# Hybrid decoder step on one core: order of the opening (warm-up, sample and memory rows, turns)

## The chip, the cores and the metric

The kernel runs on 1 core of one Trainium2 chip. Its time is the device time of the execution in microseconds (us). Before the change it takes 1202.28 us, the median of 3 runs (1201.06 to 1202.86). The execution that was profiled took 1203.43 us, of which the profile's span covers 1201.6 us.

Names of the engines: PE is TensorE (PEld its weight loads), DVE is VectorE, ACT is ScalarE, POOL is GpSimd, SP is SyncE. SPq, ACTq and POOLq are their instruction streams where these issue DMAs.

## The reference

One layer of inference for 256 prompt rows with 16 memory ("meta") rows ahead of them, and for 8 sample rows of running sequences, all of 1024 columns in float32:

```
hp = concatenate([meta, x_prompt]);  hs = x_sample
u  = rmsnorm(h, norm_mix)
q, k, v, g, p, ga, gb = split(u @ w_in)            # w_in: 1024 x 5632
q, k = rotary(q), rotary(k) * dk ** -0.5
o, S_new = retention(q, k, v, S0)                  # 4 heads, chunks of 128
ya = (silu(g) * groupnorm(o)) @ w_ret_branch
yb = (pool_mix(p) @ pool_w * pool_scale) @ w_pool_branch
h  = h + (sigmoid(ga) * ya + sigmoid(gb) * yb) @ w_out
t  = rmsnorm(h, norm_ffn)
h  = h + sum over the top 4 of 32 experts of gate * ((up + 1) * glu(gate_part)) @ w_down
y  = rmsnorm(h, norm_final)
```

The outputs are the prompt's and the samples' rows, and the new retention and pooling states. The 32 experts hold 1024 x 2048 and 1024 x 1024 float32 weights each, about 400 MB, all of which are read.

## The kernel before, in words

All instructions are written out by hand, a block for each engine, with semaphores between the blocks; no scheduler moves anything. The order in which an engine's instructions stand in its block is the order in which it runs them.

The kernel has three stages. In the opening, three tiles of token rows are loaded into `tok`: `tok[:, 0]` and `tok[:, 1]` are the prompt's 2 x 128 rows, and `tok[0:24, 2]` the 8 sample and the 16 memory rows, the "few" rows (`few = NS + NM` is 24). TensorE turns them, 128 columns at a time, by a transpose against the identity `ident` (the first part of `consts`). ScalarE scales the turned prompt rows with `norm_mix` into `x_raw` (L1414, `raw_scaled`), VectorE does the same with the turned few rows (L1693, `few_scaled`). Beside that VectorE takes the row statistics of all three tiles (L1687, L1697) for the root mean squares, which are multiplied in later.

Then comes the mixer. Its projections and branches are 72 tiles of TensorE work (`for n in range(T_END)`), of 8 matmuls each (L1016), which take their weights from 4 units of SBUF that SP fills (L630; the first unit comes in two halves, L622 and L630). Tile n = 0 is the first with real work: its first matmul waits for `raw_scaled` (the first scaled prompt block), `few_scaled` and `part_in` (the first half of the first weights).

The last stage is the mixture of experts: 16 pairs of experts in a loop, whose weights stream through a ring of 9 slots in SBUF. SP issues the next load of a slot when TensorE has used what was in it (`used`, L670 before a load at L573, L576, L581).

What sets the order in the opening:
- SP issues the two prompt loads (L605), waits for `cleared` to reach 2, issues the sample and the memory rows (L607, L608), and then the weights (L622, L630).
- ScalarE issues the early constants with the identity (L1403) and four loads of small weights (L1405); then it runs a one-element Sqrt (L1409), ahead of which the activation table is loaded.
- GpSimd clears memory: `small`, `y_sums`, `tok[:, 2]` (1024 columns), `place`, `k_few` (128 columns), `q_only`. `cleared` counts the first and the third of them; `few_cleared` counts `k_few` first.
- TensorE waits for `few_cleared`, runs WARM = 6 matmuls on the cleared `k_few` whose result nobody reads (L938), waits for the identity, and then turns the prompt tile 0 (L945), `norm_mix` (L951), the prompt tile 1 (L945), and the few rows (L954).

Of the kernel before, what the change touches and what calls it, by code (L numbers as in the profile page):

```python
# [33 lines left out]
ALU = mybir.AluOpType  # L34
# [3 lines left out]
P = 128  # L38
D = 1024
KD = D // P  # L40
WARM = 6
NPR, NS, NM = 256, 8, 16
NT = NPR + NS
NA = NT + NM
# [219 lines left out]
def build(nc, ins, outs):  # L264
    x_prompt, x_sample, state_ret, state_pool, meta = (
        ins[n] for n in ("x_prompt", "x_sample", "state_ret", "state_pool", "meta_tokens"))
    y_prompt, y_sample, ret_prompt, pool_prompt, ret_sample, pool_sample = outs

    with ExitStack() as ctx:
# [21 lines left out]
        x_raw = ring[:, 0:KD * NA].rearrange("p (k t) -> p k t", k=KD)  # L291
# [45 lines left out]
        ident, ones = const("ident"), const("ones")  # L337
# [4 lines left out]
        norm_mix, gn_w, pool_scale, norm_ffn = (params[:, a:b] for a, b in ((0, 8), (8, 16), (16, 20), (20, 28)))  # L342
# [34 lines left out]
        tok = vk[:, 0:3 * D].rearrange("p (t d) -> p t d", t=3)  # L377
# [4 lines left out]
        v_few, k_few, k_meta = small_rows[:, 0:DV], small_rows[:, DV:DV + DK], small_rows[:, DV + DK:]  # L382
# [6 lines left out]
        rows = rs[:, 0:D]  # L389
# [54 lines left out]
        psum = ctx.enter_context(nc.psum_tensor("psum", [P, 8, 512], F32))  # L444
# [4 lines left out]
        def y_tok(t):  # L449
# [7 lines left out]
        x_in = [sem(f"x_in{t}") for t in range(3)]  # L457
        ident_in, consts_in, rows_in, hist_in, misc_in, final_in = (
            sem(n) for n in ("ident_in", "consts_in", "rows_in", "hist_in", "misc_in", "final_in"))
# [6 lines left out]
        cleared, sq_done, rms_done, rstd_ready, rstd_turned = (  # L466
            sem(n) for n in ("cleared", "sq_done", "rms_done", "rstd_ready", "rstd_turned"))
        params_turned, params_ready, x_turned, u_ready, kept = (
            sem(n) for n in ("params_turned", "params_ready", "x_turned", "u_ready", "kept"))
        norm_in, norm_turned, norm_ready, few_turned, raw_scaled, few_scaled, part_in = (  # L470
            sem(n) for n in ("norm_in", "norm_turned", "norm_ready", "few_turned", "raw_scaled", "few_scaled",
                             "part_in"))
        tile_done, act_took, dve_took = sem("tile_done"), sem("act_took"), sem("dve_took")
        aux_done, aux_took, roped = sem("aux_done"), sem("aux_took"), sem("roped")
        pooled_ready, k_meta_ready, few_cleared = (sem(n) for n in ("pooled_ready", "k_meta_ready", "few_cleared"))
# [122 lines left out]
        def _(sp):  # L598
# [4 lines left out]

            for t in range(2):
                sp.dma_start(tok[:, t, :], x_prompt[0, t * P:(t + 1) * P, :]).then_inc(x_in[t], 16)  # L605
            sp.wait_ge(cleared, 2)
            sp.dma_start(tok[0:NS, 2, :], x_sample.rearrange("b s d -> (b s) d")).then_inc(x_in[2], 16)  # L607
            sp.dma_start(tok[NS:NS + NM, 2, :], meta).then_inc(x_in[2], 16)  # L608

            def mix_chunk(i):  # L610
                kind, c = CHUNKS[i]
# [110 lines left out]
        @block.gpsimd  # L722
        def _(pool):
            step = Steps(pool, pool_step)
            nc.gpsimd.memset(small[:, 0:4], 1.0).then_inc(cleared, 1)
            nc.gpsimd.memset(y_sums, 0.0).then_inc(zeroed, 1)
            nc.gpsimd.memset(tok[:, 2, :], 0.0).then_inc(cleared, 1)
            nc.gpsimd.memset(place[:, :, :], FAR).then_inc(zeroed, 1)
            nc.gpsimd.memset(k_few[:, :], 0.0).then_inc(few_cleared, 1)
            nc.gpsimd.memset(q_only[:, :, :, :], 0.0).then_inc(few_cleared, 1)  # L730

            pool.wait_ge(wmix_in[0], 16)
# [44 lines left out]
            n = NM + NPR  # L777
# [43 lines left out]
        def _(pe):  # L821
# [119 lines left out]
            few = NS + NM  # L941
            for t in range(2):
                pe.wait_ge(x_in[t], 16)
                for k in range(KD):
                    last = pe.transpose(psum[:, 4 + k // 2, (2 * (k % 2) + t) * P:(2 * (k % 2) + t + 1) * P],  # L945
                                        tok[:, t, k * P:(k + 1) * P], ident)
                    if t == 1:
                        last.then_inc(x_turned, 1)
                if t == 0:
                    pe.wait_ge(norm_in, 16)  # L950
                    pe.transpose(psum[:, 2, 0:KD], rows[0:KD, 0:P], ident[0:KD, 0:KD]).then_inc(norm_turned, 1)  # L951
            pe.wait_ge(x_in[2], 32)
            for k in range(KD):
                last = pe.transpose(psum[:, 3, k * few:(k + 1) * few], tok[0:few, 2, k * P:(k + 1) * P],  # L954
                                    ident[0:few, 0:few])
            last.then_inc(few_turned, 1)

            def turn_roots():

# [9 lines left out]
            for n in range(T_END):  # L969
                if n >= 3:  # L970
                    wait_taken(pe, n - 3)
                o = psum[:, n % 3]
# [13 lines left out]
                elif n < T_YA:  # L986
                    d = n - T_YB
                    i, cols, x, width, nk = C_PB + d // 4, (d % 4) * P, pooled, NT, PG
                    w = unit(8 + i % MIX_SLOTS).rearrange("p (k n) -> p k n", k=PG)
                else:  # L990
                    d = n - (T_YA if n < T_OUT else T_OUT)
# [407 lines left out]
        def _(act_e):  # L1399
# [1 line left out]
            A = nc.scalar.activation  # L1401

            act_e.dma_start(consts[:, 0:EARLY], ins["consts"][:, 0:EARLY]).then_inc(ident_in, 16)  # L1403
            for o, name, n in ((0, "norm_mix", 8), (8, "ret_gn", 8), (16, "pool_scale", 4), (20, "norm_ffn", 8)):
                act_e.dma_start(rows[o:o + n, 0:P], ins[name].rearrange("l (a p) -> (l a) p", p=P)).then_inc(  # L1405
                    rows_in if o else norm_in, 16)

            act_e.wait_ge(cleared, 1)
            step(A(small[:, 1:2], small[:, 0:1], ACT.Sqrt))  # L1409

            act_e.wait_ge(norm_ready, 1)
# [182 lines left out]
        def _(dve):  # L1594
            V = nc.vector
# [88 lines left out]
            for t in range(2):  # L1684
# [3 lines left out]
                if t == 0:  # L1688
                    dve.wait_ge(norm_turned, 1)
                    V.tensor_copy(norm_mix, psum[:, 2, 0:KD]).then_inc(norm_ready, 1)  # L1690
            dve.wait_ge(norm_ready, 1)
            dve.wait_ge(few_turned, 1)
            V.tensor_tensor(x_raw[:, :, NPR:NA], psum[:, 3, 0:KD * few].rearrange("p (k c) -> p k c", k=KD),  # L1693
                            norm_mix.rearrange("p (k c) -> p k c", c=1).broadcast_to([P, KD, few]),
                            ALU.mult).then_inc(few_scaled, 1)
            for n in range(2):
                step(V.bn_stats(row_stats[:, 2, n], tok[:, 2, n * 512:(n + 1) * 512]))  # L1697
            step.wait()
# [370 lines left out]
```

## Time and profile before

| | |
|---|---|
| time, median of 3 runs | 1202.28 us (1201.06 to 1202.86) |
| time of the profiled execution | 1203.43 us |
| its span | 1201.6 us |
| PE busy | 1154.7 us, 96% |
| PE weight loads | 572.8 us, 48% |
| DVE, ACT, POOL busy | 307.2, 160.0, 62.8 us |
| chain that ended last | PE 68%, DMA 30%, SPq 1% |
| DMA over the span | 455.09 MB, mean 379 GB/s |

The busy times are shares of the whole span and say little of a stage of 9 us. For the opening the useful views are the chain of waits (what released what, up to the last instruction) and the timeline (each engine's instructions in order of time); for the rest, a table by stretches, which gives each engine's busy time, TensorE's granted clock (PEclk, 1.00 is full speed) and the share and rate of the DMA engines. In these views "idle 0.57 <-DMA ..." says that the engine had stood still for 0.57 us and what is taken to have released it.

### The profile page before, as it was taken

What the parts mean: (1) busy time and instruction counts of PE and PEld (TensorE: products, weight loads), DVE (VectorE), ACT (ScalarE), POOL (GpSimd) and SP (SyncE); (2) the same over time, 40 slices, a digit from 0 to 9 for tenths busy, and PEclk for the clock granted to TensorE, in tenths of its full rate; (3) what the DMA queues carried; (4) which work ended last, traced back from release to release, by engine and by line L of the source; (5) the groups of instructions that cost most, each with busy time, mean ns of one, the idle gap of its engine ahead of it and who ended that gap; (6) DMA issues with size and microseconds to landing.
All of it is one profiled execution on the core that took longest, in us unless ns stands there. A gap on an engine that the chain in (4) does not pass through costs nothing.

```text
span 1201.6 us, 13661 instructions
## 1 busy us (share of the span) xinstructions
PE 1154.7 (96%) x5403; PEld 572.8 (48%) x5403; DVE 307.2 (26%) x699; ACT 160.0 (13%) x314; POOL 62.8 (5%) x92
## 2 busy tenths in 40 slices
PE   8999999999999999999989998989999989999997
PEld 7888788886434334333434333434333434333332
DVE  4363511232122122221221221213121212121222
ACT  2122111002010111111110101010101100110112
POOL 3252600000000000000000000000000000000000
PEclk9999999999999999999999999999999999999999
DMA  9762788476999999999999999999999999999996
GB/s 321 231 228 90 261 327 319 142 315 264 424 418 427 424 434 428 425 434 425 425 434 426 431 428 434 421 435 426 436 425 433 421 433 429 433 428 429 428 419 241
DMA packets 63728, 455.09 MB, mean 379 GB/s; under 512 B 4321, under 2 KB 35501, under 8 KB 42688
## 3 DMA queue, kind: packets, MB, share of 16 engines
q1 hardware_dynamic: 59168, 439.60, 88.3%
q0 software_dynamic: 4176, 14.34, 3.5%
q8 instruction: 27, 0.44, 0.2%
q10 hardware_dynamic: 344, 0.61, 0.1%
q14 instruction: 13, 0.11, 0.0%
HBM read 448.65 MB, written 6.11 MB: 378 GB/s over the span
## 4 chain that ended last, share of the span: by engine, by line
PE 68%; DMA 30%; SPq 1%; issue 0%; ACT 0%; DVE 0%; DVEq 0%; ACTq 0%
PE psum L1087 24%; DMA ring<-in_w_down 21%; PE psum L1016 19%; PE psum L1098 10%; DMA ring<-in_w_gate_up 8%; PE psum L1174 5%; PE psum L1208 2%; PE psum L1154 1%; SPq L591 1%; PE psum L1164 1%; PE psum L1209 1%; PE psum L1183 1%; DMA ring<-in_x_prompt 0%; PE psum L897 0%; PE psum L1088 0%
## 5 line engine op out<-in xcount | busy, mean ns | idle before, releaser
L1087 PE MATMUL psum<-ring,x_T 128*64 128x512 f32 x1004 | 455.7, 600 | 9.6 <-DMA ring<-in_w_gate_up 8.8
L1088 PE MATMUL psum<-ring,x_T 128*64 128x512 f32 x994 | 450.6, 600 | 0.0
L1087 PEld LDWEIGHTS psum<-ring,x_T 128*64 128x64 f32 x1004 | 131.0, 137 | 275.1 <-issue 252.4
L1098 PE MATMUL psum<-ring,act_T 128*64 128x512 f32 x960 | 216.0, 602 | 25.1 <-DMA ring<-in_w_down 25.1
L1016 PE MATMUL psum<-ring 128*128 128x264 f32 (+1 forms) x768 | 181.7, 392 | 0.6 <-DMA ring<-in_w_in 0.6
L1016 PEld LDWEIGHTS psum<-ring 128*128 128x128 f32 x768 | 143.2, 190 | 30.2 <-ACT qk L1445 2.1
L1098 PEld LDWEIGHTS psum<-ring,act_T 128*64 128x64 f32 x960 | 70.2, 138 | 159.4 <-issue 139.6
L1088 PEld LDWEIGHTS psum<-ring,x_T 128*64 128x64 f32 x994 | 129.6, 137 | 0.0
L1906 DVE TENSOR_TENSOR h_raw<-psum,params 128x512 f32<-128x512 f32 x32 | 22.1, 691 | 295.0 <-PE psum L1154 295.0
L1923 DVE TENSOR_TENSOR z_T<-z_T,psum 128x264 f32<-128x264 f32 x112 | 43.0, 425 | 205.5 <-PE psum L1209 205.5
L1174 PE MATMUL psum<-normed,one_hot 128*128 128x512 f32 x168 | 74.4, 592 | 0.0
L1504 ACT ACTIVATE h_raw<-h_raw 128x512 f32<-128x512 f32 x32 | 20.2, 631 | 251.5 <-DVE h_raw L1909 251.5
L1487 ACT COPY h_raw<-psum 128x512 f32<-128x512 f32 x32 | 18.8, 586 | 224.5 <-PE psum L1088 224.5
L1174 PEld LDWEIGHTS psum<-normed,one_hot 128*128 128x128 f32 x168 | 30.9, 190 | 33.5 <-issue 33.5
L1154 PEld LDWEIGHTS psum<-consts,h_raw 128*128 128x128 f32 x256 | 33.6, 211 | 26.4 <-issue 26.0
L1918 DVE SCALAR_TENSOR_TENSOR act_T<-h_raw 128x512 f32<-128x512 f32 x30 | 20.8, 692 | 91.5 <-PE psum L1098 84.0
L1208 PEld LDWEIGHTS psum<-hot_T,out_hi 128*128 128x128 f32 x112 | 21.0, 187 | 45.4 <-issue 45.4
L1496 ACT COPY h_raw<-psum 128x512 f32<-128x512 f32 x28 | 16.4, 586 | 183.0 <-PE psum L1174 183.0
L1154 PE MATMUL psum<-consts,h_raw 128*128 128x128 f32 x256 | 40.1, 298 | 0.0
L1825 DVE TENSOR_TENSOR x_T<-psum,small 128x256 f32<-128x256 f32 x64 | 25.5, 420 | 52.8 <-PE psum L1164 27.3
L1208 PE MATMUL psum<-hot_T,out_hi 128*128 128x264 f32 x112 | 35.4, 336 | 0.0
L1209 PE MATMUL psum<-hot_T,out_lo 128*128 128x264 f32 x112 | 29.4, 283 | 0.0
(268 smaller groups left out, 751.3 us busy)
## 6 DMA issues: line engine op xcount, KB each, us to landing
ring<-in_w_gate_up SPq DMA_DIRECT2D x32, 4096.0 KB, 31.7
ring<-in_w_gate_up SPq DMA_DIRECT2D x59, 2048.0 KB, 29.8
ring<-in_w_down SPq DMA_DIRECT2D x56, 2048.0 KB, 33.3
ring<-in_w_in SPq DMA_DIRECT2D x21, 1024.0 KB, 6.6
ring<-in_w_down SPq DMA_DIRECT2D x12, 1024.0 KB, 26.8
spare<-in_w_gate_up SPq DMA_DIRECT2D x5, 1280.0 KB, 36.8
out<-ring POOLq DMA_DIRECT2D x9, 512.0 KB, 9.5
ring<-in_state_ret POOLq DMA_DIRECT2D x8, 512.0 KB, 7.2
```

The source lines that it names most:

```text
L1016: last = mm(o[:, 0:width], w[:, k, cols:cols + P], x[:, k, 0:width], start=k == 0, stop=k == nk - 1)
L1087: mm(psum[0:CAP, 2 * j + n], x, gate, start=first, stop=final)
L1088: last = mm(psum[CAP:P, 2 * j + n], x, up, start=first, stop=final)
L1098: last = mm(psum[j * CAP:(j + 1) * CAP, 4 + n], hidden[:, j, 4 * h + i], w, start=h == 0 and i == 0, stop=h == 1 and i == 3)
L1154: last = pe.transpose(psum[:, 6 + m // 4, (m % 4) * P:(m % 4 + 1) * P], h_raw[:, f0:f0 - m % 4 + 4 * P:4], ident)
L1174: last = mm(psum[:, bank + n], one_hot[:, t].rearrange("p j c -> p (j c)"), normed[:, t, n * 512:(n + 1) * 512], start=t == 0, stop=t == 2)
L1208: mm(o, out_hi[:, c], hot_T[:, :], start=True, stop=False)
L1209: mm(o, out_lo[:, c], hot_T[:, :], start=False, stop=True).then_inc(scattered, 1)
L1825: return V.tensor_tensor(x_T[:, k, j], psum[:, 4 + half].rearrange("p (k j c) -> p k j c", k=4, j=2)[:, :, j], ffn_pairs[:, k].rearrange(" ...
L1906: V.tensor_tensor(hg, turned[:, :, 0], bias(e, 0), ALU.add).then_inc(gate_biased, 1)
L1918: V.scalar_tensor_tensor(hidden[:, j], hu, 1.0, hs, ALU.add, ALU.mult).then_inc(act_ready, 1)
L1923: V.tensor_tensor(y_T[:, d], y_T[:, d], psum[:, 6 + d % 2, 0:NT], ALU.add).then_inc(y_added, 1)
```

## The change

- WARM goes from 6 to 10 matmuls, and GpSimd clears `k_few`, for which they wait, first of all instead of fifth. `tok[:, 2]` is cleared third as before, but behind `k_few` and `small` instead of `small` and `y_sums`.
- The sample and the memory rows are loaded from ScalarE's stream, behind the constants and `norm_mix`, instead of from SP's, ahead of the weights. ScalarE waits there for `cleared` to reach 2, and issues its three other small loads behind them.
- TensorE turns the few rows between the two prompt tiles instead of behind both, and VectorE scales them between the statistics of the two prompt tiles instead of behind both.

```diff
-WARM = 6
+WARM = 10
@@ SP
             for t in range(2):
                 sp.dma_start(tok[:, t, :], x_prompt[0, t * P:(t + 1) * P, :]).then_inc(x_in[t], 16)
-            sp.wait_ge(cleared, 2)
-            sp.dma_start(tok[0:NS, 2, :], x_sample.rearrange("b s d -> (b s) d")).then_inc(x_in[2], 16)
-            sp.dma_start(tok[NS:NS + NM, 2, :], meta).then_inc(x_in[2], 16)
@@ GpSimd
+            nc.gpsimd.memset(k_few[:, :], 0.0).then_inc(few_cleared, 1)
             nc.gpsimd.memset(small[:, 0:4], 1.0).then_inc(cleared, 1)
+            nc.gpsimd.memset(tok[:, 2, :], 0.0).then_inc(cleared, 1)
             nc.gpsimd.memset(y_sums, 0.0).then_inc(zeroed, 1)
-            nc.gpsimd.memset(tok[:, 2, :], 0.0).then_inc(cleared, 1)
             nc.gpsimd.memset(place[:, :, :], FAR).then_inc(zeroed, 1)
-            nc.gpsimd.memset(k_few[:, :], 0.0).then_inc(few_cleared, 1)
             nc.gpsimd.memset(q_only[:, :, :, :], 0.0).then_inc(few_cleared, 1)
@@ TensorE, in the loop over the two prompt tiles
                 if t == 0:
                     pe.wait_ge(norm_in, 16)
                     pe.transpose(psum[:, 2, 0:KD], rows[0:KD, 0:P], ident[0:KD, 0:KD]).then_inc(norm_turned, 1)
-            pe.wait_ge(x_in[2], 32)
-            for k in range(KD):
-                last = pe.transpose(psum[:, 3, k * few:(k + 1) * few], tok[0:few, 2, k * P:(k + 1) * P],
-                                    ident[0:few, 0:few])
-            last.then_inc(few_turned, 1)
+                    pe.wait_ge(x_in[2], 32)
+                    for k in range(KD):
+                        last = pe.transpose(psum[:, 3, k * few:(k + 1) * few], tok[0:few, 2, k * P:(k + 1) * P],
+                                            ident[0:few, 0:few])
+                    last.then_inc(few_turned, 1)
@@ ScalarE
-            for o, name, n in ((0, "norm_mix", 8), (8, "ret_gn", 8), (16, "pool_scale", 4), (20, "norm_ffn", 8)):
-                act_e.dma_start(rows[o:o + n, 0:P], ...).then_inc(rows_in if o else norm_in, 16)
-
-            act_e.wait_ge(cleared, 1)
+            act_e.dma_start(rows[0:8, 0:P], ins["norm_mix"]...).then_inc(norm_in, 16)
+            act_e.wait_ge(cleared, 2)
+            act_e.dma_start(tok[0:NS, 2, :], x_sample.rearrange("b s d -> (b s) d")).then_inc(x_in[2], 16)
+            act_e.dma_start(tok[NS:NS + NM, 2, :], meta).then_inc(x_in[2], 16)
+            for o, name, n in ((8, "ret_gn", 8), (16, "pool_scale", 4), (20, "norm_ffn", 8)):
+                act_e.dma_start(rows[o:o + n, 0:P], ...).then_inc(rows_in, 16)
             step(A(small[:, 1:2], small[:, 0:1], ACT.Sqrt))
@@ VectorE, in the loop over the two prompt tiles
                 if t == 0:
                     dve.wait_ge(norm_turned, 1)
                     V.tensor_copy(norm_mix, psum[:, 2, 0:KD]).then_inc(norm_ready, 1)
-            dve.wait_ge(norm_ready, 1)
-            dve.wait_ge(few_turned, 1)
-            V.tensor_tensor(x_raw[:, :, NPR:NA], ...).then_inc(few_scaled, 1)
+                    dve.wait_ge(norm_ready, 1)
+                    dve.wait_ge(few_turned, 1)
+                    V.tensor_tensor(x_raw[:, :, NPR:NA], ...).then_inc(few_scaled, 1)
```

On TensorE, at the program's start, the order before is this; the 128x24 matmuls are the turns of the few rows, the 128x280 ones are the first projections:

```order
1 L938 MATMUL psum<-ring 128x128 x6
2 L945 MATMUL psum<-consts,ring 128x128 x8
3 L951 MATMUL psum<-consts,ring 128x8
4 L945 MATMUL psum<-consts,ring 128x128 x8
5 L954 MATMUL psum<-consts,ring 128x24 x8
6 L1016 MATMUL psum<-ring 128x280 x16
```

And this is the order in the changed kernel, where each line number is 3 lower:

```order
1 L935 MATMUL psum<-ring 128x128 x10
2 L942 MATMUL psum<-consts,ring 128x128 x8
3 L948 MATMUL psum<-consts,ring 128x8
4 L951 MATMUL psum<-consts,ring 128x24 x8
5 L942 MATMUL psum<-consts,ring 128x128 x8
6 L1013 MATMUL psum<-ring 128x280 x16
```

The eight turns of the few rows have moved ahead of the second prompt tile, with their wait for the rows' landing, and four warm-up matmuls are new.

On ScalarE, at the program's start, the stream before is this:

```order
1 L1403 DMA consts<-in_consts 128x132
2 L1405 DMA ring<-in_norm_mix 8x128
3 L1405 DMA ring<-in_ret_gn 8x128
4 L1405 DMA ring<-in_pool_scale 4x128
5 L1405 DMA ring<-in_norm_ffn 8x128
6 L1409 ACT_TABLE_LOAD
7 L1409 ACTIVATE small<-small 128x1
8 L1414 ACTIVATE ring<-psum,params 128x256 x8
```

And this is the changed kernel's:

```order
1 L1400 DMA consts<-in_consts 128x132
2 L1401 DMA ring<-in_norm_mix 8x128
3 L1403 DMA ring<-in_x_sample 8x1024
4 L1404 DMA ring<-in_meta_tokens 16x1024
5 L1406 DMA ring<-in_ret_gn 8x128
6 L1406 DMA ring<-in_pool_scale 4x128
7 L1406 DMA ring<-in_norm_ffn 8x128
8 L1408 ACT_TABLE_LOAD
```

Two more DMAs are issued ahead of the table load, and both rows' loads stand behind the constants and `norm_mix`.

## Rows read from the trace of the kernel before

**Rows 1.** Chain of waits, 0 to 80 us: start us, us, what.

```profile
1.21 5.58 DMA ring<-in_x_prompt
...
6.84 1.09 PE psum L945 x8
7.93 0.60 PE psum L954 x8
...
9.10 7.79 PE psum L1016 x32
```

**Rows 2.** Timeline, 0 to 11 us: start us, us, engine, line, instruction, idle before.

```profile
0.75 0.10 POOL L725 MEMSET small<- 128x4 f32 x1 [0.29 <-POOLq L2061]
0.75 0.89 SPq L605 DMA_DIRECT2D ring<-in_x_prompt  x2
...
0.81 0.95 POOL L727 MEMSET ring<- 128x1024 f32 x1
...
1.79 0.34 SPq L607 DMA_DIRECT2D ring<-in_x_sample  x1
1.83 0.21 POOL L729 MEMSET ring<- 128x128 f32 x1
2.09 2.93 PE L938 MATMUL psum<-ring 128*128 128x128 f32 x12 [2.09 <-POOL ring L729]
...
2.18 0.33 SPq L608 DMA_DIRECT2D ring<-in_meta_tokens  x1
2.55 0.47 SPq L622 DMA_DIRECT2D ring<-in_w_in  x1
...
4.14 0.20 ACT L1409 ACTIVATE small<-small 128x1 f32<-128x1 f32 x1
4.97 1.29 DVE L1687 BATCH_NORM_STATS2 first_stats<-ring 128x6 f32<-128x512 f32 x2 [4.97 <-DMA ring<-in_x_prompt]
...
5.16 1.27 PE L945 MATMUL psum<-consts,ring 128*128 128x128 f32 x8
...
6.37 0.22 PE L951 MATMUL psum<-consts,ring 8*128 8x8 f32 x1
...
7.38 3.03 ACT L1414 ACTIVATE ring<-psum,params 128x256 f32<-128x256 f32 x8 [3.04 <-PE psum L945]
...
7.86 0.57 PEld L954 LDWEIGHTS psum<-consts,ring 24*128 24x128 f32 x8 [0.17 <-issue]
...
8.64 0.36 DVE L1693 TENSOR_TENSOR ring<-psum,params 128x192 f32<-128x192 f32 x1 [0.54 <-PE psum L954]
...
9.10 7.79 PE L1016 MATMUL psum<-ring 128*128 128x280 f32 x32 [0.57 <-DMA ring<-in_w_in]
```

**Rows 3.** The issue at L622 alone, and its time from issue to landing.

```profile
L622 SPq DMA_DIRECT2D ring<-in_w_in x1: 466/466/466, 2.5 to 2.5; - x1
DMA to landing us min/median/max: 6.0/6.0/6.0
```

**Rows 4.** DMA issues of 0 to 30 us: KB each, median us to landing.

```profile
consts<-in_consts ACTq DMA_DIRECT2D x1, 66.0 KB, 4.4
```

**Rows 5.** Warm-up and scaling alone: durations ns min/median/max, first and last start us.

```profile
L938 PE MATMUL psum<-ring x12: 421/421/582, 2.1 to 4.6; 128*128 128x128 f32 x12
L1414 ACT ACTIVATE ring<-psum,params x8: 468/488/516, 7.4 to 9.9; 128x256 f32<-128x256 f32 x8
```

**Rows 6.** By stretches: us, PE, PEld, DVE, ACT, POOL busy, PEclk, DMA share, GB/s.

```profile
5.50:6.50 1.00, 1.00 (x9) 0.83 (x7) 0.75 (x2) 0.00 (x0) 0.00 (x0) 1.00 1.03 237
6.50:9.00 2.50, 1.78 (x17) 1.42 (x16) 1.81 (x5) 1.62 (x5) 0.00 (x0) 1.00 1.08 343
260.00:280.00 20.00, 19.88 (x112) 16.31 (x110) 7.50 (x29) 4.05 (x6) 0.00 (x0) 0.91 0.65 263
285.00:290.00 5.00, 5.00 (x26) 1.60 (x24) 0.57 (x3) 0.00 (x0) 0.00 (x0) 1.00 0.32 82
300.00:1180.00 880.00, 845.41 (x3887) 330.36 (x3885) 201.48 (x437) 102.66 (x189) 0.00 (x0) 0.99 1.01 428
```

More of the change, by code:

```diff
@@ L1403, in _ @@
             act_e.dma_start(consts[:, 0:EARLY], ins["consts"][:, 0:EARLY]).then_inc(ident_in, 16)
-            for o, name, n in ((0, "norm_mix", 8), (8, "ret_gn", 8), (16, "pool_scale", 4), (20, "norm_ffn", 8)):
-                act_e.dma_start(rows[o:o + n, 0:P], ins[name].rearrange("l (a p) -> (l a) p", p=P)).then_inc(
-                    rows_in if o else norm_in, 16)
-            act_e.wait_ge(cleared, 1)
+            act_e.dma_start(rows[0:8, 0:P], ins["norm_mix"].rearrange("l (a p) -> (l a) p", p=P)).then_inc(norm_in, 16)
+            act_e.wait_ge(cleared, 2)
+            act_e.dma_start(tok[0:NS, 2, :], x_sample.rearrange("b s d -> (b s) d")).then_inc(x_in[2], 16)
+            act_e.dma_start(tok[NS:NS + NM, 2, :], meta).then_inc(x_in[2], 16)
+            for o, name, n in ((8, "ret_gn", 8), (16, "pool_scale", 4), (20, "norm_ffn", 8)):
+                act_e.dma_start(rows[o:o + n, 0:P], ins[name].rearrange("l (a p) -> (l a) p", p=P)).then_inc(rows_in, 16)
             step(A(small[:, 1:2], small[:, 0:1], ACT.Sqrt))
@@ L1690, in _ @@
                     V.tensor_copy(norm_mix, psum[:, 2, 0:KD]).then_inc(norm_ready, 1)
-            dve.wait_ge(norm_ready, 1)
-            dve.wait_ge(few_turned, 1)
-            V.tensor_tensor(x_raw[:, :, NPR:NA], psum[:, 3, 0:KD * few].rearrange("p (k c) -> p k c", k=KD),
-                            norm_mix.rearrange("p (k c) -> p k c", c=1).broadcast_to([P, KD, few]),
-                            ALU.mult).then_inc(few_scaled, 1)
+                    dve.wait_ge(norm_ready, 1)
+                    dve.wait_ge(few_turned, 1)
+                    V.tensor_tensor(x_raw[:, :, NPR:NA], psum[:, 3, 0:KD * few].rearrange("p (k c) -> p k c", k=KD),
+                                    norm_mix.rearrange("p (k c) -> p k c", c=1).broadcast_to([P, KD, few]),
+                                    ALU.mult).then_inc(few_scaled, 1)
             for n in range(2):
```

## The prediction

> **What bounds the kernel now.** I read the chain of waits first, then the timeline of the first 11 us, and then the table by stretches, because the change touches only the opening and the question is whether what happens there reaches the end.
>
> In the chain [rows 1] the reader sees that the opening hangs on the second prompt load: it lands at 6.79 us, TensorE turns tile 1 from 6.84 to 7.93 and the few rows to 8.53, stands still for 0.57 us and starts the projections at 9.10. From there TensorE works without a stop: the first two tiles of the projection take 7.79 us. What ended the 0.57 us has to be worked out. The view names the weights' DMA, but its landing was at 2.55 + 6.0 = 8.55 us [rows 2, 3], half a microsecond too early. VectorE's scaling of the few rows ran from 8.64 to 9.00 [rows 2], and TensorE started 0.10 us after it. ScalarE's first scaled block was done much sooner: it began at 7.38 and one takes 0.49 us, so 7.87 [rows 2, 5]. So three things had to be there, at 7.87, 8.55 and 9.00 us, and the few rows' scaling was the last.
>
> The rest of the program falls in two parts. The mixer up to about 280 us is TensorE's (19.88 us busy of 20 from 260 to 280), and from 285 to 290 the DMA engines are busy for only 0.32 of the time, because they wait for TensorE to free slots. From 300 to 1180 us the DMA share is 1.01 at 428 GB/s [rows 6]: the weights' stream is the limit. The stream's start, however, hangs on TensorE's progress through the mixer. So what the opening gains or loses moves the stream, and with it the end, by the same amount; I cost this passing-on at one for one.
>
> **The change part by part.**
>
> *SP's stream.* Two issues go, 0.34 and 0.33 us with their gaps. L622 was issued at 2.55 us, behind the row loads at 1.79 and 2.18, and the two prompt loads were issued from 0.75 to 1.64. So L622 moves to about 1.67, that is 0.88 us sooner [rows 2]. Does the landing move as much? At most: 8.55 - 0.88 = 7.67 us. At least hardly at all, since the transfers stand behind 1 MB of prompt rows of the same queue and the DMA engines are full (share 1.03 from 5.5 to 6.5). But the rate there is only 237 GB/s against 343 in the next stretch [rows 6], so something other than bytes holds the beginning of these transfers up. I take 0.3 us sooner, 8.25, nearer to no movement; the ends are 7.67 and 8.55.
>
> The Trainium skill, "DMA: Bandwidth & Descriptors", section "Issuing engines are not separate DMA queues", says that issuing from several engines saves only the issuing time, since all use the same 16 DMA engines. By that rule the gain is the issue time of SP alone and the bytes are not faster; by the trace the issue is worth 0.88 us at most, and whether it counts is open.
>
> *The rows on ScalarE's stream.* `tok[:, 2]` is cleared behind `k_few` (0.21 us) instead of behind `small` and `y_sums`; the clearing of 0.95 us began at 0.81 and begins now near 1.0, so it ends near 1.95 [rows 2]. The two loads are issued at 2.0 and 2.35 us, 0.2 us later than before, done near 2.7. They are no longer behind the prompt rows in SP's queue but behind the constants. When they land, no row of before shows. The nearest rows are the constants, 4.4 us from issue to landing on this queue [rows 4], and the weights, 6.0 us [rows 3]. Counted from 2.7 these give 7.1 and 8.7 us. The two loads are 24 rows of 4 KB, 96 KB in all, which could as well land in 4 us like the prompt tile 0 of 512 KB, which VectorE had at 4.97 us [rows 2]. I take 6.7, ends 6.2 and 8.7. Against the prompt they cost something: 96 KB at 343 GB/s [rows 6] are 0.28 us, which tile 1 can land later than 6.79, so 7.07.
>
> The Trainium skill, same page, section "Queues, rings and completion order", says each DMA engine goes round the queues that have work, packet by packet. By that rule the rows are not held up by the prompt's bytes ahead of them, and the prompt pays for it; the trace of before has no 4 KB rows on ScalarE's queue that would test it.
>
> The three small loads of ScalarE behind them slip by some 0.9 us, and so does the table load: the Sqrt ended at 4.34 and ends now near 5.3. ScalarE's next work was at 7.38 [rows 2], so 2 us of its idle time cover it. If that cover were gone the whole 0.9 would count.
>
> *The warm-up.* It waits for `k_few`, cleared now at 0.75 + 0.21 = 0.96 us instead of 2.04, and starts at 1.0 instead of 2.09. Each fp32 matmul is two passes in the trace; 12 passes started between 2.1 and 4.6 us [rows 5], 0.23 us apart. Twenty passes keep TensorE until 1.0 + 20 x 0.22 = 5.4 us, if they run at the pace of before. Tile 0 was begun at 5.16 [rows 2], so it starts about 0.25 us later. The passes took 421 ns each while the turns of the same shape came at a quicker pace, so the engine still ran at the lower of its two levels in the warm-up; longer work before tile 0 can bring the rise forward and give the 0.25 us back, but nothing here shows it.
>
> *The turns.* Before, tile 0 from 5.16, `norm_mix` at 6.37, then waiting until 6.79 for tile 1. Now tile 0 from 5.4, `norm_mix` at 6.6, the few rows at 6.85 if they have landed (0.57 us of weight loads), tile 1 from 7.4. Tile 1 was turned from 6.84 and ScalarE followed at 7.38, 0.54 us behind [rows 1, 2]. So ScalarE begins at 7.95 and its first block is there at 8.44 [rows 5]. VectorE has the turned few rows at 7.6 and is done at 8.0.
>
> *Sum.* The three conditions of the first projection become 8.44 (was 7.87), 8.25 (was 8.55) and 8.0 (was 9.00). The last is now ScalarE's first block, and TensorE starts at 8.5 instead of 9.10: 0.6 us sooner. The ends: 7.9 with all well (the clock rises early, the rows land at 6.2: 1.2 us sooner), and, with the rows landed at 8.7, 8.7 + 0.57 + 0.54 + 0.49 + 0.1 = 10.4, 1.3 us later. Nothing behind it turns late: ScalarE makes a block every 0.38 us (3.03 / 8), TensorE uses one in 0.49 (7.79 / 16) [rows 1, 2].
>
> In the profiled execution that is 1203.43 - 0.6 = 1202.8 us. The median of the runs shown lies 1.15 below that execution, so I forecast 1202.28 - 0.6, **1201.7 us**.
>
> **The rivals.**
>
> *Nothing moves.* The weights' first half is held by bytes and lands at 8.5 as before, and the rows come near 7.3. TensorE then starts between 8.7 and 9.1. For it: DMA share 1.03 and 1.08 in these stretches [rows 6]. Against it: the few rows' scaling at 9.00 was later than both other conditions and does go. Gain 0 to 0.4, time 1202.1.
>
> *The rows block tile 1.* TensorE runs in order, so the wait for the few rows now stands ahead of tile 1, of ScalarE's eight blocks and of VectorE's statistics. The path from their landing to the start is 0.57 + 0.54 + 0.49 + 0.1 = 1.7 us, so from a landing later than 9.10 - 1.7 = 7.4 us the change loses. At 8.7 us it loses 1.3, time 1203.6. If TensorE's clock falls in that longer pause, there is more: from 260 to 280 us the granted clock was 0.91 [rows 6], which is 0.09 x 20 = 1.8 us of full-speed work lost; 1.3 + 1.8 = 3.1, time 1205.4. For it: the constants needed 4.4 us on this very queue. Against it: prompt tile 1, issued at 1.21 and 5 times larger, was there in 5.6 us.
>
> *The clock is worth more than the order.* The profiled execution is only one. If in others TensorE is still at its lower level when the projections begin, a longer warm-up mends that. For it: the three runs lie 1.8 us apart, and the warm-up's passes did run at the lower level. Against it: the same spread can come from the 880 us of streaming, of which 0.2% is already as much. Gain 0.6 + up to 1.8, 1199.9 to 1201; with 1.2 it is 1200.5.
>
> **How the numbers follow.** Forecast (0.3 to 1.2 sooner) 0.60; nothing moves 0.16; rows block tile 1 0.13, of which 0.04 with the clock; clock worth more 0.11, of which 0.07 go past the bound. A difference under 0.2%, 2.4 us, can't be told from none. So faster 0.07, slower 0.04, the same 0.89. The range takes the forecast's ends (1201.1 and 1202.0), then the spread of the runs, 1.2 down and 0.6 up from their median, and half of the clock's 1.8 on either side: 1199.8 to 1203.4.
>
> **What would show it.** Right: the first L1016 matmul (L1013 there) starts between 8.2 and 8.8 us; the warm-up starts near 1.0 and ends near 5.5; SP's first weight issue at 1.7; the Sqrt ends before ScalarE's first block; VectorE's scaling of the few rows ends by 8.1, and the whole chain is shifted alike at 280 us. Wrong: TensorE idle between `norm_mix` and the few rows beyond 7.4 us; a start of the projections at 9.1 or later; a gap at the fifth matmul of the first tile, where the second half of the weights is asked for; a gain at 9 us that is gone at 300 us, which would break the one-for-one passing-on.

## The result, and the profile after

The changed kernel takes 1204.24 us, the median of 20 runs (1202.26 to 1205.99), against 1202.19 us (1201.06 to 1202.96, 20 runs) before. The ratio is 1.0016, 95% interval 1.001 to 1.0022: about 2 us slower. The forecast was 1201.7 with a range up to 1203.4, so it was wrong in its sign, and the time lies outside the range. A second measurement of the same kernel, told below, gave 1.0025 (1.0015 to 1.0034).

The chain of waits of the changed kernel, 0 to 20 us (start us, us, what), answers to [rows 1]:

```profile
1.91 0.28 ACTq L1403
2.19 0.03 issue
2.22 6.11 DMA ring<-in_meta_tokens
8.33 0.04 issue
8.38 0.79 PE psum L951 x8
9.17 1.90 PE psum L942 x8
11.06 8.16 PE psum L1013 x32
19.22 0.77 PE psum L960 x6
```

The opening no longer hangs on the second prompt tile but on the memory rows. Their DMA was issued at 2.22 us on ScalarE's queue and landed at 8.33, 6.11 us later. TensorE stood still for it, with tile 1 behind it in its stream. The projections start at 10.86 us in the timeline below instead of 9.10 (the chain counts them from 11.06, when tile 1 is through), and their first two tiles end at 19.22 instead of 16.89. That is 2.33 us later, more than the start by 0.57.

The timeline of the changed kernel shows the same on each engine, and answers to [rows 2]:

```profile
1.00 4.56 PE L935 MATMUL psum<-ring 128*128 128x128 f32 x20 [1.00 <-POOL ring L722]
...
1.68 0.43 SPq L619 DMA_DIRECT2D ring<-in_w_in  x1
...
5.39 1.04 PE L942 MATMUL psum<-consts,ring 128*128 128x128 f32 x8
...
6.36 0.22 PE L948 MATMUL psum<-consts,ring 8*128 8x8 f32 x1
...
8.37 0.67 PEld L951 LDWEIGHTS psum<-consts,ring 24*128 24x128 f32 x8 [1.88 <-DMA ring<-in_meta_tokens]
...
9.10 1.97 PE L942 MATMUL psum<-consts,ring 128*128 128x128 f32 x8
...
9.28 0.36 DVE L1692 TENSOR_TENSOR ring<-psum,params 128x192 f32<-128x192 f32 x1 [2.49 <-PE psum L951]
...
9.89 3.02 ACT L1413 ACTIVATE ring<-psum,params 128x256 f32<-128x256 f32 x8 [4.56 <-PE psum L942]
...
10.86 8.37 PE L1013 MATMUL psum<-ring 128*128 128x280 f32 x32
```

The reader sees the pause in front of L951, 1.88 us, and that tile 1 (at 9.10) now takes 1.97 us for the eight turns that took 1.09 before [rows 1]. Tile 0 had taken 1.04. The by-stretch table (us, PE, PEld, DVE, ACT, POOL busy, PEclk, DMA share, GB/s) says why; it answers to [rows 6]:

```profile
6.00:8.50 2.50, 0.71 (x7) 0.46 (x6) 0.35 (x2) 0.00 (x0) 0.00 (x0) 1.00 1.10 272
8.50:10.00 1.50, 1.50 (x12) 1.45 (x13) 0.72 (x2) 0.11 (x1) 0.00 (x0) 0.59 1.10 348
10.00:12.50 2.50, 2.50 (x10) 2.10 (x10) 2.43 (x8) 2.50 (x8) 1.26 (x2) 0.56 1.10 349
12.50:19.00 6.50, 6.50 (x29) 5.28 (x28) 3.00 (x8) 1.08 (x4) 0.00 (x0) 1.00 1.09 330
260.00:280.00 20.00, 20.00 (x125) 16.51 (x124) 7.00 (x27) 2.83 (x5) 0.00 (x0) 1.00 0.65 261
```

TensorE worked for 0.71 of the 2.5 us up to 8.50, and its granted clock was then 0.59 and 0.56 on average until 12.50: it had fallen to the lower of its two levels, 1.2 GHz instead of 2.4, for most of these 4 us, and was back at 1.00 behind them. Before, the column read 1.00 through the whole opening. It does so even during the warm-up, where TensorE was slow: these 20 passes took 4.56 us, 0.23 each, while the 8 unread passes of e9, told below, took 1.16 at 7 us, 0.15 each. So until the engine first runs at full pace, 1.00 in this column says nothing.

The weights' first half did not come sooner either: issued at 1.68 instead of 2.55 us, it took 7.1 us instead of 6.0 [rows 3], and landed at 8.8 instead of 8.55.

```profile
DMA to landing us min/median/max: 7.1/7.1/7.1
```

### The profile page after: what moved, and what is told of

The parts are those of the page before. It is cut to its first block, busy times and chain, and to the rows that moved or that the text cites. A ratio compares the mean times of both kernels' runs of the same rounds, so it can differ in the third digit from the quotient of the medians.

```text
span 1202.3 us, 13677 instructions
## 1 busy us (share of the span) xinstructions
PE 1155.6 (96%) x5411; PEld 575.4 (48%) x5411; DVE 307.3 (26%) x699; ACT 159.6 (13%) x314; POOL 62.6 (5%) x92
## 3 DMA queue, kind: packets, MB, share of 16 engines
HBM read 448.65 MB, written 6.11 MB: 378 GB/s over the span
## 4 chain that ended last, share of the span: by engine, by line
PE 67%; DMA 30%; SPq 1%; issue 0%; ACT 0%; DVE 0%; POOL 0%; ACTq 0%; DVEq 0%; POOLq 0%
PE psum L1084 23%; DMA ring<-in_w_down 22%; PE psum L1013 19%; PE psum L1095 11%; DMA ring<-in_w_gate_up 8%; PE psum L1171 5%; PE psum L1205 1%; PE psum L1151 1%; PE psum L1161 1%; SPq L591 1%; PE psum L1206 1%; PE psum L1180 1%; DMA ring<-in_meta_tokens 1%; PE psum L894 0%; PE psum L1085 0%
```

## The experiments

Eleven experiments ran, one of them the changed kernel again. A useful mark in each profile is the start of the 10.88 us stretch of three projection tiles near the mixer's end, since TensorE does not stop between the opening and there; it stood at 258.32 us before and at 260.67 in the changed kernel.

```profile
258.32 10.88 PE psum L1016 x48
```

```profile
260.67 10.88 PE psum L1013 x48
```

So 2.35 us separate the two, the 2.33 of the opening within rounding. The table holds what the profile of each kernel shows, and beside it the ratio of the times, whose interval is some 1 us either way. A mark is sharp, but it is that of one execution: the changed kernel was profiled twice, and its two marks differ by 0.65 us. So marks of a few tenths, taken from one profile each, show which way a change points and no more. The starts are those of the timelines.

| kernel | memory rows landed | projections start | mark against before | ratio (95%) |
|---|---|---|---|---|
| before | by 7.86 | 9.10 | 0 | 1 |
| changed | 8.33 | 10.86 | +2.35 | 1.0016 (1.0010 to 1.0022) |
| e8, changed again | 8.59 | 10.39 | +3.00 | 1.0025 (1.0015 to 1.0034) |
| e1, warm-up alone | by 8.20 | 9.45 | +0.36 | 1.0001 (0.9988 to 1.0013) |
| e2, rows on SP | 7.0 | 8.79 | -0.30 | 1.0003 (0.9993 to 1.0012) |
| e3, turned last | 8.5 | 9.82 | +2.42 | 1.0007 (0.9998 to 1.0016) |
| e4, 5 fillers | 8.4 | 10.21 | +1.12 | 1.0013 (1.0004 to 1.0022) |
| e9, 4 fillers | 8.39 | 10.19 | +1.10 | 1.0016 (1.0007 to 1.0025) |
| e4b, 7 fillers | before 9.12 | 10.88 | +1.79 | 1.0017 (1.0008 to 1.0026) |
| e5, rows on GpSimd | 8.89 | 10.84 | +2.98 | 1.0019 (1.0011 to 1.0028) |
| e6, constants on SP | 7.5 | 9.39 | +0.33 | 1.0003 (0.9994 to 1.0011) |
| e7, turned in tile 1 | by 7.48 | 8.79 | -0.37 | 0.9994 (0.9985 to 1.0003) |
| e10, the same, 8 warm-ups | 7.08 | 8.44 | -0.64 | 0.9995 (0.9986 to 1.0004) |

**e1, the warm-up alone.** The kernel before, with

```diff
-WARM = 6
+WARM = 10
+            nc.gpsimd.memset(k_few[:, :], 0.0).then_inc(few_cleared, 1)
             nc.gpsimd.memset(small[:, 0:4], 1.0).then_inc(cleared, 1)
-            nc.gpsimd.memset(k_few[:, :], 0.0).then_inc(few_cleared, 1)
```

> The kernel before with the warm-up's part of the change alone (k_few cleared first, ten matmuls). My theory, that the loss comes from the few rows landing late ahead of tile 1 and from the clock that falls in that pause: projections start at 9.1 us as before, granted clock 1.00 from 6 to 19 us, time within 0.4 us of before. Rival, the longer warm-up itself is the loss (it delays tile 0 or makes the granted clock fall later on): start later than 9.5 us or a clock under 1.00 before 19 us, and 1 to 2 us slower.

The ratio was 1.0001 (0.9988 to 1.0013). In its timeline:

```profile
1.00 4.64 PE L938 MATMUL psum<-ring 128*128 128x128 f32 x20 [1.00 <-POOL ring L725]
...
5.43 1.66 PE L945 MATMUL psum<-consts,ring 128*128 128x128 f32 x8
...
7.17 1.09 PE L945 MATMUL psum<-consts,ring 128*128 128x128 f32 x8
...
9.45 7.79 PE L1016 MATMUL psum<-ring 128*128 128x280 f32 x32 [0.57 <-issue]
```

Ten warm-ups keep TensorE until 5.43, tile 0 starts 0.27 us late and was still slow in this execution (1.66 us), so that tile 1 was begun at 7.17 instead of 6.84 and the start slipped by 0.35. The warm-up alone brought nothing and cost little: with a mark at +0.36 it is not the loss of 2.35. From 8.5 to 19 us the clock was 1.00. The start at 9.45 is later than my 9.1, and just short of the rival's 9.5.

**e2, the rows back on SP's queue.** The changed kernel, with

```diff
+            sp.wait_ge(cleared, 2)
+            sp.dma_start(tok[0:NS, 2, :], x_sample...).then_inc(x_in[2], 16)
+            sp.dma_start(tok[NS:NS + NM, 2, :], meta).then_inc(x_in[2], 16)
@@ ScalarE
-            act_e.wait_ge(cleared, 2)
-            act_e.dma_start(tok[0:NS, 2, :], x_sample...).then_inc(x_in[2], 16)
-            act_e.dma_start(tok[NS:NS + NM, 2, :], meta).then_inc(x_in[2], 16)
+            act_e.wait_ge(cleared, 1)
```

> The changed kernel with the sample and memory rows' two loads put back into SP's stream, behind the prompt and ahead of the weights; warm-up and the turn between the two tiles stay. Theory (ScalarE's queue makes the rows late): they land near 7.3 us, TensorE idles at most 0.7 us, projections start at 8.9 to 9.1, clock 1.00, time 0 to 0.3 us under before. Rival (turning the few rows between the tiles costs by itself, whoever loads them): rows at 8 us or later, start after 10 us, 1.5 to 2 us slower than before.

Ratio 1.0003 (0.9993 to 1.0012), and in the timeline:

```profile
2.28 0.33 SPq L608 DMA_DIRECT2D ring<-in_meta_tokens  x1
...
5.06 1.09 PE L945 MATMUL psum<-consts,ring 128*128 128x128 f32 x8
...
7.03 0.57 PEld L954 LDWEIGHTS psum<-consts,ring 24*128 24x128 f32 x8 [0.81 <-DMA ring<-in_meta_tokens]
...
8.79 7.79 PE L1016 MATMUL psum<-ring 128*128 128x280 f32 x32
```

Issued at about the same time as in the changed kernel, but behind the prompt on SP's queue, the rows were there at 7.0 instead of 8.33 us. All came a little sooner than expected (7.3 us, start 8.9 to 9.1), and the turn between the tiles gives 0.3 us. This takes the loss away by undoing one part, so the moved loads are its cause. That part holds two things: the rows leave ScalarE's queue, and they are issued ahead of the weights again (SP issues the first weights at 2.65 us instead of 1.68). No run separates them; a kernel with the rows on ScalarE's queue and the weights held back behind them would, and was not run.

**e3, the few rows turned last again.** The changed kernel with TensorE's turn and VectorE's scaling of the few rows put back behind both prompt tiles:

```diff
-                    pe.wait_ge(x_in[2], 32)      (in the loop, behind norm_mix)
+            pe.wait_ge(x_in[2], 32)              (behind the loop, with its eight turns; the same on VectorE)
```

> The changed kernel with the few rows turned and scaled behind both prompt tiles, as before; their loads stay on ScalarE's queue. Theory: rows land at 8.3 us, tile 1 is turned from 6.9 to 8.0 meanwhile, the few rows to 9.0, scaled at 9.6, start at 9.7 with the clock at 1.00; 0.6 us slower than before. Rival (the place of the turn doesn't matter, the late rows cost the same wherever they are waited for): start at 10.5 or later, 2 us slower.

Ratio 1.0007 (0.9998 to 1.0016), near the 0.6 us expected; the start at 9.82 is near the 9.7 expected. But the clock was not at 1.00 in the profiled execution, which was the slowest of the kernel's eleven runs (1205.38 us, median 1203.03):

```profile
6.11 1.09 PE L942 MATMUL psum<-consts,ring 128*128 128x128 f32 x8
...
8.58 0.57 PEld L951 LDWEIGHTS psum<-consts,ring 24*128 24x128 f32 x8 [1.62 <-DMA ring<-in_meta_tokens]
...
9.82 9.47 PE L1013 MATMUL psum<-ring 128*128 128x280 f32 x32 [0.57 <-issue]
```

The first two projection tiles took 9.47 us instead of 7.79: 1.7 us for one fall of the clock behind a pause of 1.6 us. This execution was 2.35 us over the kernel's median, and it also had the other fall, of 1.50 us, told in the last section. So at least one of the two was missing in most of its runs, and which one is not known; the forecast of 1.00 for the opening missed in the one execution that was seen. By the way tile 1 was turned at 6.11, 0.7 us sooner than before. Whether the prompt lands sooner because the few rows are gone from its queue was not tried; with them on it, e10 began tile 1 at 6.51.

**e4, e9 and e4b, TensorE kept at work in the pause.** The changed kernel, with unread matmuls ahead of the wait:

```diff
+                    for _ in range(5):
+                        mm(psum[:, 7, 0:P], k_few, k_few, start=True, stop=True)
                     pe.wait_ge(x_in[2], 32)
```

In e4 they write over a part of the turned prompt tile 0 in PSUM, so that its computation differs in those columns; e9 (four) and e4b (seven) write to bank 1 and leave all as it is.

> The changed kernel with five more unread 128x128 matmuls between the turn of norm_mix and the wait for the few rows, so that TensorE works through the pause. Theory, that about half of the loss is the clock: rows at 8.3 us as before it, granted clock 1.00 from 8.5 to 12.5 us, projections start at 10.1 to 10.4 and their first two tiles take 7.8 us; 1.1 us slower than before, 0.9 faster than the changed kernel. Rival (the wait alone is the loss): the clock may be up, but the time is the changed kernel's within 0.3 us.

> The changed kernel with seven unread 128x128 matmuls in the pause ahead of the few rows (into a PSUM bank that holds nothing yet). Measured so far: with a filler the projections start at 10.21 us and run at full clock, the first two tiles done at 18.0 us, against 19.2 in the changed kernel and 16.9 before. Theory (the opening passes on one for one): 1.1 us slower than before, 0.9 to 1.2 faster than the changed kernel's 2.05. Rival (the time lost is not the opening's): 2 us slower although the opening is 1.2 us shorter.

> The changed kernel with four unread matmuls in the pause, short enough to end before the rows land. Theory (of the 2 us about one is the clock): projections start at 10.0 to 10.3 us at full clock, first two tiles done at 18.0, 1.0 to 1.3 us slower than before, 0.8 to 1.2 faster than the changed kernel beside it. Rival (the clock costs nothing in the whole time): the same time as the changed kernel within 0.3 us.

In e9's timeline:

```profile
6.98 1.16 PE L950 MATMUL psum<-ring 128*128 128x128 f32 x8
...
8.43 0.57 PEld L953 LDWEIGHTS psum<-consts,ring 24*128 24x128 f32 x8 [0.49 <-DMA ring<-in_meta_tokens]
...
9.04 1.09 PE L942 MATMUL psum<-consts,ring 128*128 128x128 f32 x8
...
10.19 7.79 PE L1015 MATMUL psum<-ring 128*128 128x280 f32 x32
```

The rows came as late as ever, but the clock was 1.00 in all four stretches from 6 to 19 us, tile 1 took 1.09 and the projections 7.79. The mark stood at +1.10 and in e4 at +1.12, against +2.35 and +3.00 without fillers. So of the changed kernel's delay at the mark 1.1 us is the wait. The rest is 1.25 us in its first profile and 1.90 in its second (e8), where 0.20 us are the rows' later landing; that leaves 1.2 to 1.7 us for the clock.

In the times this gain does not show. e9's ratio 1.0016 lies below the 1.0025 of the changed kernel measured beside it (medians 1204.24 and 1205.04, the intervals overlap), but it equals the 1.0016 of that kernel's first 20 runs. The traces say where the gain can go: all three kernels with fillers had the other fall of the clock, behind the mark (last section), and neither profile of the changed kernel had it. SP's first load for the experts behind it was issued at 288.50 us in the changed kernel's first profile, and here at

```profile
288.76 3.76 SPq L576 DMA_DIRECT2D ring<-in_w_gate_up  x2
```

The 1.25 us won at the mark were gone 29 us later. So the rival of e4's forecast, that the clock may be up and the time the same, is not ruled out, and the 0.8 to 1.2 us expected of e9 were not shown.

e4b missed: its seven fillers began at 7.36, since the warm-up and tile 0 had been slow in that execution, and held TensorE until 9.12, beyond the rows' landing; the mark +1.79 fits the ratio 1.0017. It does not test what I sent it for.

**e5, the rows on GpSimd's queue.**

```diff
             nc.gpsimd.memset(tok[:, 2, :], 0.0).then_inc(cleared, 1)
+            pool.wait_ge(cleared, 2)
+            pool.dma_start(tok[0:NS, 2, :], x_sample...).then_inc(x_in[2], 16)
+            pool.dma_start(tok[NS:NS + NM, 2, :], meta).then_inc(x_in[2], 16)
```

> The changed kernel with the few rows' two loads issued by GpSimd right behind its own clearing. Theory, that the rows are late because they stand behind the constants and norm_mix on ScalarE's queue: on another queue they land by 7.0 us and the projections start by 9.0; time within 0.5 us of before. Rival, that any second queue is starved beside the prompt and the weights: landing at 8 us or later, start after 10 us, 1 to 2 us slower.

The rival's numbers held: landing at 8.89 us, start at 10.84. The chain:

```profile
2.82 6.07 DMA ring<-in_meta_tokens
```

Only the sample rows stood ahead of the memory rows on that queue, and they still took 6.07 us, against 6.11 on ScalarE's and 4.7 (2.28 to 7.0) on SP's. Projections from 10.84 in 9.01 us, with the clock at 0.51 from 10 to 12.5 us, ratio 1.0019. Two things keep it from being a clean test of "any second queue": the profile lists this queue as another kind (software_dynamic, the other two are hardware_dynamic), and SP's weights were still issued ahead of the rows, at 1.68 us.

**e6, the constants off ScalarE's queue.**

```diff
                 sp.dma_start(tok[:, t, :], x_prompt...).then_inc(x_in[t], 16)
+                if t == 0:
+                    sp.dma_start(consts[:, 0:EARLY], ins["consts"][:, 0:EARLY]).then_inc(ident_in, 16)
@@ ScalarE
-            act_e.dma_start(consts[:, 0:EARLY], ins["consts"][:, 0:EARLY]).then_inc(ident_in, 16)
```

> The changed kernel with the early constants issued by SP between the two prompt tiles; ScalarE's queue then holds norm_mix, the few rows and the three small loads. Theory (backlog of the constants' 128 small rows on ScalarE's queue): rows land by 6.5 us, identity by 5.5, start at 8.5 to 9.0 us, 0.3 us faster than before. Rival (a queue beside SP's gets its transfers late whatever stands ahead of them): rows land at 8 us or later, 1 to 2 us slower.

```profile
2.14 0.43 SPq L621 DMA_DIRECT2D ring<-in_w_in  x1
...
2.23 0.34 ACTq L1405 DMA_DIRECT2D ring<-in_meta_tokens  x1
...
7.59 0.57 PEld L953 LDWEIGHTS psum<-consts,ring 24*128 24x128 f32 x8 [0.56 <-DMA ring<-in_meta_tokens]
...
9.39 7.81 PE L1015 MATMUL psum<-ring 128*128 128x280 f32 x32
```

Between the two: the rows landed near 7.5 us, 5.3 after the issue. That is 0.8 us sooner than in the changed kernel, of which not all need be the constants: SP issued the weights 0.46 us later here (2.14 against 1.68). And ScalarE's queue still takes 0.6 us longer than SP's. Here the weights, landed at 2.14 + 7.20 = 9.34 us, set the start. The packets by queue tell where the time went. In the changed kernel ScalarE's queue (q10) moved nothing from 4.6 to 5.5 us, while SP's (q1) moved 0.34 MB, and the 0.10 MB of the rows, issued by 2.6 us, ran from 5.5 to 7.5. In e6, with no constants ahead, q10 had moved 0.07 MB of them by 5.5. So the rows' first bytes start late behind the constants, and their last ones are slow beside the weights in both. Why a queue beside SP's takes longer is left open. In the profiles of before, of the changed kernel and of e1, e2 and e3 the DMA engines are full between 6 and 7 us (shares 1.02 to 1.14) at only 252 to 264 GB/s, when the weights' small pieces begin; whether that is the reason was not tried.

**e7 and e10, the rows turned inside tile 1.** From the kernel before (rows on SP's queue), with e1's warm-up; the few rows are turned behind tile 1's first two turns, and VectorE scales them between tile 1's two statistics. e10 is the same with WARM = 8.

```diff
                     if t == 1:
                         last.then_inc(x_turned, 1)
+                    if t == 1 and k == 1:
+                        pe.wait_ge(x_in[2], 32)
+                        for j in range(KD): (the turns of the few rows)
+                        last.then_inc(few_turned, 1)
```

> The kernel before (rows on SP's queue) with the longer warm-up, and the few rows turned behind the first two turns of tile 1, whose scaling ScalarE starts at once. Theory: rows there by 7.1 us, tile 1's first two turns from 6.9, few rows turned by 7.9, start at 8.6 to 8.8, which the weights' landing (8.3 to 8.6) bounds; 0.3 to 0.5 us faster than before, not to be told from none. Rival (the start is bound by the weights' landing near 8.6 or the bytes): start between 8.9 and 9.4 as in the kernel before.

> The version with the few rows on SP's queue turned inside tile 1 (the one with ten warm-up matmuls started the projections at 8.79 us), now with eight. Theory, that ten overrun the identity's landing and push tile 1 from 6.8 to 7.1: tile 0 starts at 5.1, the projections at 8.5 to 8.7, 0.4 to 0.6 us faster than before. Rival, that eight end too early for the clock: granted clock under 1.00 between 6 and 13 us and a time 0 to 1 us over before.

e10's timeline:

```profile
4.90 1.52 PE L945 MATMUL psum<-consts,ring 128*128 128x128 f32 x8
...
6.51 0.44 PE L945 MATMUL psum<-consts,ring 128*128 128x128 f32 x2
...
7.12 0.57 PEld L952 LDWEIGHTS psum<-consts,ring 24*128 24x128 f32 x8 [0.41 <-DMA ring<-in_meta_tokens]
...
8.44 7.80 PE L1017 MATMUL psum<-ring 128*128 128x280 f32 x32
```

ScalarE's first two blocks go ahead and the few rows' wait hides behind them. The start moves to 8.79 and 8.44 us (expected 8.6 to 8.8, and 8.5 to 8.7), the mark to -0.37 and -0.64 us, both near what was expected. The ratios, 0.9994 and 0.9995, point the same way with 1 inside their intervals. By the mark it is the better kernel, in one profile each and by no more than two profiles of one kernel can differ (0.65 us); by the times it is not to be told from before.

**e8, the changed kernel again.**

> The changed kernel itself once more, for a second profile and beside e9 on one chip. Theory, that the late rows and the fall of the clock in the pause both recur: rows land at 8.2 to 8.4 us, granted clock under 1.00 somewhere between 8 and 13 us, the projections' first two tiles done at 18.8 to 19.3 us, 2 us slower than before. Rival, that the fall in the first profile was a chance of that execution: clock 1.00 to 19 us, first two tiles done at 17.9 to 18.2, time 1 to 1.3 us over before in most runs.

```profile
8.63 0.57 PEld L951 LDWEIGHTS psum<-consts,ring 24*128 24x128 f32 x8 [1.22 <-DMA ring<-in_meta_tokens]
...
9.24 1.09 PE L942 MATMUL psum<-consts,ring 128*128 128x128 f32 x8
...
10.39 9.47 PE L1013 MATMUL psum<-ring 128*128 128x280 f32 x32
```

The rows were late again (2.22 + 6.37 = 8.59 us) and the clock fell again, this time later: tile 1 took its full-speed 1.09 us and the projections 9.47. The mark was +3.00, the ratio 1.0025. The landing (expected by 8.4) and the end of the two tiles (19.86, expected by 19.3) were later than I had said. The rival is gone: the fall came in both profiles of this kernel, and its place moved. It begins between 8.5 and 9 us in the first and between 10.5 and 11 here, when TensorE had been at work again for about 2 us.

## Why the prediction was wrong

The chain was read rightly: before, the few rows' scaling, done at 9.00, was the last condition. In e1 it was done at 9.35 and the projections started at 9.45, again 0.10 us behind. That the opening's loss reaches the end one for one fits as far as the times can tell: in the changed kernel the mark has moved by 2.35 us and the time by 2.05 (20 runs), and in e8 by 3.00 and about 3.0. Between mark and end the clock's other fall can come in between (e9).

The step that failed is "The rows on ScalarE's stream". It put their landing at 6.7 us, with ends 6.2 and 8.7; it was 8.33 and 8.59, near the far end. The issue was costed well (2.22 us, against 2.35). What failed is the time from issue to landing. The 6.7 is 4.0 us behind the end of the issue at 2.7, or 4.35 behind its start: the figure of prompt tile 0 and of the constants (4.4 us), which were issued first, when the DMA engines had nothing else. It measured 6.11 from the start of the issue. The nearest row was the weights' 6.0 us [rows 3], issued at nearly the same time as the rows; with it the sum gives 2.35 + 6.0 = 8.35 and the slower outcome. I had the row and used it only for the far end. That the two figures agree so well is in part luck, since the weights themselves then took 7.1 us.

"The rows block tile 1" was the rival that came true, with a chance of 0.13, of which 0.04 with the clock. Its working holds: from landing to start 1.7 us, so 8.33 + 1.7 = 10.0, and e9 started at 10.19 with the rows at 8.39, which is 1.8. Its clock term, 1.8 us, was 1.2 to 1.7. The wait (1.1 us) and the clock add up to what the mark moved. The chance looks too small, above all for the clock, since a pause of nearly 2 us directly ahead of the work was plain once the landing was set late. The range did not hold this rival either: it ended at 1203.4, below the 1203.6 and 1205.4 that the rival gave, so 0.13 of the chances lay outside it. Its ends were also added up wrongly: from the terms named they are 1201.1 - 1.2 - 0.9 = 1199.0 and 1202.0 + 0.6 + 0.9 = 1203.5, not 1199.8 and 1203.4. The measured time lies outside either.

"SP's stream": I took the weights 0.3 us sooner between ends 7.67 and 8.55. They landed at 8.8, outside both. The issue came 0.87 us sooner and the transfer took 1.1 us longer. The rule of the Trainium skill, "DMA: Bandwidth & Descriptors", section "Issuing engines are not separate DMA queues", that issuing from several engines saves only the sequencer's time, agrees with the trace as far as it goes: the bytes came no sooner. Here even the 0.87 us of issuing that were saved were worth nothing at the landing. The prediction also drew on the Trainium skill, "DMA: Bandwidth & Descriptors", section "Queues, rings and completion order", by which each DMA engine takes the queues in turn, packet by packet. What I concluded from it, that the rows would not be held up off SP's queue, is not borne out as a gain: there they came 1.3 us later (e2 against the changed kernel).

"The warm-up" was sized rightly (start 1.00, tile 0 from 5.39, expected 5.4), and e1 shows it as a loss of 0.35 us in the opening, not as a gain, in one execution in which tile 0 was also slow (1.66 us). "The turns" were right too: with the rows there in time (7.0 us, e2) the order gives 0.3 us, where the sum had 0.6. The rival "the clock is worth more" found no support: before, in e1 and in e2 the clock was at its full level when the projections began.

## What to carry to other kernels

A small load that is moved to another queue and awaited earlier is not priced by its bytes: take the issue-to-landing time of what is issued beside it under the same load (here 6.0 us, against 6.11 measured), not of what was issued first (4.4). A wait moved ahead on an in-order engine should stand behind work that other engines are already waiting for (e7, e10), and a pause that it may open on TensorE is to be priced with the clock's fall, which at the mark cost as much as the pause itself. For changes under 0.2% a mark in the profile behind the changed part tells more than the times, but it wants more than one profile of each kernel (0.65 us between two here) and a second mark further on, since a gain at the first can be gone at the second (e9).

## What was not expected of the hardware

TensorE's clock also fell once between the mixer and the experts, in 6 of the 13 profiles, and no pause stood before it. In the profile of before TensorE was busy without a stop from 19 us on; from 271.6 to 274.3 it ran four groups of six matmuls of only 32 or 1 columns, then 24 turns (L1039), and the clock fell at about 275. In the profile before, the granted clock from 260 to 280 us was 0.91 [rows 6], in the changed kernel's 1.00. From the mark to SP's next load, which waits for TensorE's first expert work, it was 287.65 - 258.32 = 29.33 us before and 288.50 - 260.67 = 27.83 after:

```profile
287.65 3.76 SPq L576 DMA_DIRECT2D ring<-in_w_gate_up  x2
```

```profile
288.50 3.76 SPq L576 DMA_DIRECT2D ring<-in_w_gate_up  x2
```

The 1.50 us are that fall's price. The same step is 29.33 or 29.34 us in all six profiles with the fall (before, e2, e3, e4, e4b and e9) and 27.83 or 27.84 in all seven without it. What decides whether it comes is open. It came behind openings at full clock and behind one with a fall (e3), but in all three kernels with fillers and in neither profile of the changed one.

It explains why the two profiled executions lie only 0.84 us apart (1203.43 and 1204.27) though their openings differ by 2.33 us: 2.33 - 1.50 = 0.83. That the figures meet so closely is luck. From the load at 287.65 and 288.50 to the end it was 915.8 us in both, but over the thirteen profiled executions it was 914.3 to 916.8, so the experts' stream adds 2.5 us of spread of its own. How much of the 1.8 us between the three first runs is this fall, and how much the stream, is not known.
